# A mixture-of-experts block on one core: the light job of each pair first, the first job's flags counted early, the table inside job 0

## The reference

```python
def grouped_moe(x, w_router, router_bias, w_gate, w_up, w_down):
    scores = jax.nn.sigmoid((x @ w_router).astype(jnp.float32))
    ...
    gates = chosen / jnp.sum(chosen, axis=-1, keepdims=True)
    combine = jnp.einsum('btk,btke->bte', gates, jax.nn.one_hot(idx, N_EXPERTS, dtype=jnp.float32)).astype(x.dtype)
    y = jnp.zeros_like(x)
    for e in range(N_EXPERTS):
        h = jax.nn.silu(x @ w_gate[e]) * (x @ w_up[e])
        y = y + combine[..., e:e + 1] * (h @ w_down[e])
    return y
```

## Time and profile before

| | before |
|---|---|
| runs | 1537.62 us median of 3 (1533.61 to 1541.21) |
| the profiled execution | 1539.95 us, span 1538.0 us |
| granted TensorE clock, mean over the span | 0.924 |
| instructions recorded | 19449 |
| TensorE busy | 1301.7 us (85%) |
| VectorE, ScalarE, GpSimd busy | 430.4, 143.8, 76.2 us |
| moved by DMA | 559.43 MB, mean 364 GB/s |

### The profile page before, as it was taken

One profiled execution on the slowest core, in us unless ns is written; L12 is line 12 of the kernel. 1 busy time (PEld: TensorE's weight loads), 2 busy tenths in 40 slices (PEclk: granted clock), 3 DMA queues, 4 the chain that ended last, 5 costly groups with the idle time before them and its releaser, 6 DMA issues.

```text
span 1538.0 us, 19449 instructions
## 1 busy us (share of the span) xinstructions
PE 1301.7 (85%) x7868; PEld 540.2 (35%) x7869; DVE 430.4 (28%) x808; ACT 143.8 (9%) x252; POOL 76.2 (5%) x138
## 2 busy tenths in 40 slices
PE   3899999899998989799899899786787688687666
PEld 2556544455454564233233233122122122122121
DVE  3213694767557150012011111111111110101102
ACT  3000101323100123000000000000000000000000
POOL 0112100111131000000000000000000000000000
PEclk9999999899999879899999899998898898898867
DMA  9999668556888559879999999999999999999995
GB/s 373 420 388 409 259 261 336 183 203 234 317 346 298 203 196 422 340 285 399 422 422 422 421 422 421 422 421 421 421 422 422 422 422 422 421 422 421 422 420 245
DMA packets 84355, 559.43 MB, mean 364 GB/s; under 512 B 9680, under 2 KB 9680, under 8 KB 22608
## 3 DMA queue, kind: packets, MB, share of 16 engines
q1 hardware_dynamic: 69408, 502.49, 80.1%
q0 software_dynamic: 14320, 52.01, 9.2%
q10 hardware_dynamic: 576, 4.19, 0.7%
HBM read 556.57 MB, written 2.10 MB: 363 GB/s over the span
## 4 chain that ended last, share of the span: by engine, by line
PE 46%; DMA 44%; DVE 4%; issue 2%; ACT 2%; SPq 1%; DVEq 0%; ACTq 0%; POOL 0%
DMA ring<-w_gate_dram 16%; DMA ring<-w_up_dram 16%; PE ps L831 7%; PE ps L568 7%; PE ps L826 7%; DMA rope_heads<-w_down_dram 5%; PE ps L671 3%; DMA ring<-w_half_dram 3%; PE ps L858 3%; DMA ring<-w_in_dram 3%; PE ps L562 3%; PE ps L852 2%; PE ps L801 2%; PE ps L573 2%; PE ps L789 1%
## 5 line engine op out<-in xcount | busy, mean ns | idle before, releaser
L826 PE MATMUL ps<-ring,early 128*32 128x256 f32 x2304 | 179.4, 448 | 75.9 <-DMA ring<-w_gate_dram 32.3
L831 PE MATMUL ps<-ring,early 128*64 128x512 f32 x672 | 165.0, 613 | 27.8 <-DMA ring<-w_gate_dram 18.2
L1509 DVE TENSOR_TENSOR big<-ps,big 128x1024 f32<-128x1024 f32 x64 | 75.4, 1220 | 324.4 <-PE ps L789 324.4
L568 PE MATMUL ps<-ring,big 128*128 128x512 f32 x320 | 147.0, 601 | 0.0
L826 PEld LDWEIGHTS ps<-ring,early 128*32 128x32 f32 x2304 | 73.1, 123 | 195.5 <-issue 64.8
L1149 DVE SCALAR_TENSOR_TENSOR halves<-ring,silu_c,halves 128x1024 f32<-128x1024 f32 x96 | 123.2, 1283 | 39.6 <-DMA ring<-w_half_dram 33.3
L671 PE MATMUL ps<-ring,big 128*128 128x512 f32 x256 | 114.5, 604 | 1.3 <-ACT big L1034 1.3
L831 PEld LDWEIGHTS ps<-ring,early 128*64 128x64 f32 x672 | 41.5, 138 | 135.4 <-issue 64.9
L568 PEld LDWEIGHTS ps<-ring,big 128*128 128x128 f32 x320 | 59.2, 192 | 69.6 <-issue 69.4
L671 PEld LDWEIGHTS ps<-ring,big 128*128 128x128 f32 x256 | 48.8, 194 | 59.8 <-issue 59.8
L789 PE MATMUL ps<-halves,early 64*128 64x512 f32 x256 | 66.8, 642 | 0.0
(11 more groups left out here) (327 smaller groups left out, 1067.5 us busy)
## 6 DMA issues: line engine op xcount, KB each, us to landing
ring<-w_gate_dram SPq DMA_DIRECT2D x128, 1024.0 KB, 26.0
ring<-w_up_dram SPq DMA_DIRECT2D x64, 1024.0 KB, 26.0
ring<-w_down_dram SPq DMA_DIRECT2D x64, 1024.0 KB, 27.2
ring<-w_half_dram POOLq DMA_DIRECT2D x96, 512.0 KB, 6.5
ring<-w_mix_dram SPq DMA_DIRECT2D x32, 1024.0 KB, 12.0
big<-w_up_dram SPq DMA_DIRECT2D x32, 1024.0 KB, 26.0
big<-w_down_dram SPq DMA_DIRECT2D x32, 1024.0 KB, 25.3
ring<-w_in_dram SPq DMA_DIRECT2D x28, 1024.0 KB, 9.2
```

The lines of the kernel that those rows point to most:

```text
L568: mm = pe.matmul(ps[:, b + t, :], nT[:, k, t * P:(t + 1) * P], w, start=(k == 0), stop=(k == KT - 1))
L826: mm = pe.matmul(out_b[0][BASE * f:BASE * (f + 1), :], rows[0][:, k, :], w[:, kk, f * 256:(f + 1) * 256], start=(k == 0), stop=(k == KT - 1))
L831: mm = pe.matmul(out_b[1][REST * f:REST * (f + 1), :], rows[1][:, k, :], w[:, kk, f * N:(f + 1) * N], start=(k == 0), stop=(k == KT - 1))
L1509: tt(y, banks[:, 2 * h:2 * h + 2, :].rearrange("p a n -> p (a n)"), y, ALU.add).then_inc(done, 1)
```

## The change

It has four parts. In each pair of jobs the few job stands in front (TensorE's loops and the numbering on VectorE are changed together). Job 0's flags few and some come from a count of their own: two more small matmuls in route step 1, two operations on VectorE into two new places of `n_i`, and a step ("kind",) behind k = 9 in which TensorE reads them into registers. The table's matmuls move out of the schedule into `experts`, between gate and up of job 0, and write to the bank T; route steps 2 and 3 stand behind k = 7 and 11. Waits move with them: SyncE's wait of chunk 11 is for cand_ready, and for table_ready only behind chunk 23; TensorE waits for table_ready after job 0; job 0 waits for two gathered blocks at each gate chunk instead of all 16 at its start; the counts of the pairs are read one by one where they are used.

```diff
--- before.py
+++ after.py
@@ -101,8 +101,10 @@
     seq += [("hT", 3), ("logits", 3), ("gate_b", 0), ("gate_b", 1), ("route", 1)]
     for k in range(KT):
         seq.append(("first", k))
-        if k in (4, 8, 12):
-            seq.append(("route", 1 + k // 4))
+        if k in (7, 11):
+            seq.append(("route", 2 if k == 7 else 3))
+        if k == 9:
+            seq.append(("kind",))
     return seq
 
 
@@ -207,7 +209,7 @@
         bufB = sb("bufB", [P, 1024])
         probs = sb("probs", [P, 2, N])
         small = sb("small", [P, 64])
-        n_i = sb("n_i", [1, 4 * JOBS + 5], I32)
+        n_i = sb("n_i", [1, 4 * JOBS + 7], I32)
         hsq = sb("hsq", [P, TT, 4])
         onehot_j = sb("onehot_j", [CAND, JOBS])
         vcol = sb("vcol", [CAND, 10])
@@ -343,7 +345,7 @@
         outs_saved = [sem("outs0_saved"), sem("outs1_saved")]
         out_ready, out_sent = sem("out_ready"), sem("out_sent")
         dve_step, spread_saved = sem("dve_step"), sem("spread_saved")
-        sort_done = sem("sort_done")
+        sort_done, first_kind = sem("sort_done"), sem("first_kind")
 
         block = stack.enter_context(nc.Block())
 
@@ -400,13 +402,14 @@
                 elif i == 10:
                     sp.wait_ge(mask_ready, 1)
                 elif i == 11:
-                    sp.wait_ge(table_ready, 1)
+                    sp.wait_ge(cand_ready, 1)
                 if i < SLOTS:
                     sp.wait_ge(slot_free, used_job(i - SLOTS))
                 elif i >= JOB_SLOTS:
                     sp.wait_ge(slot_free, used_job(i - JOB_SLOTS))
                 sp.dma_start(job_slots[i % JOB_SLOTS], weights[i // 8][FIRST_EXPERT, i % 8]) \
                     .then_inc(job_landed[i % JOB_SLOTS], 16)
+            sp.wait_ge(table_ready, 1)
             jobs = sp.value_load(n_i[0:1, 4 * JOBS:4 * JOBS + 1], min_val=2, max_val=JOBS - 1)
             with sp.Fori(1, jobs) as j:
                 e = sp.value_load(n_i[0:1, bass.ds(j, 1)], min_val=0, max_val=NE - 1)
@@ -716,6 +719,9 @@
                         for t in range(TT):
                             mm = pe.matmul(T[0:CAND, 128:129], cand[:, t, 0, :], ones[:, 0:1],
                                            start=(t == 0), stop=(t == TT - 1))
+                        for t in range(TT):
+                            pe.matmul(T[0:1, 130:131], cand[:, t, 0, FIRST_EXPERT:FIRST_EXPERT + 1], ones[:, 0:1],
+                                      start=(t == 0), stop=(t == TT - 1))
                         pe.wait_ge(shift_ready, 1)
                         pe.matmul(T[:, 2 * NE:3 * NE], ones, rt[:, 18, 0, :], start=True, stop=True).then_inc(pos_done, 1)
                     elif part == 2:
@@ -732,21 +738,11 @@
                                 mm = pe.transpose(C[0][0:CAND, (2 * t + i) * P:(2 * t + i + 1) * P],
                                                   cand[:, t, i, :], ident)
                         mm.then_inc(candT_done, 1)
-                    else:
-                        pe.wait_ge(table_oh, 2)
-                        for i in range(2):
-                            for t in range(TT):
-                                at = (i * TT + t) * JOBS
-                                pe.matmul(Z[0][:, at:at + JOBS], candT[:, t, i, :], onehot_j[:],
-                                          start=True, stop=True)
-                        pe.matmul(Z[0][0:1, 256:256 + JOBS], k_("expert")[0:CAND, :], onehot_j[:],
-                                  start=True, stop=True)
-                        pe.matmul(Z[0][0:1, 256 + JOBS:256 + 2 * JOBS], vcol[:, 3:4], onehot_j[:],
-                                  start=True, stop=True)
-                        pe.matmul(Z[0][0:1, 256 + 2 * JOBS:256 + 3 * JOBS], vcol[:, 9:10], onehot_j[:],
-                                  start=True, stop=True)
-                        pe.matmul(Z[0][0:1, 256 + 3 * JOBS:256 + 4 * JOBS], vcol[:, 4:5], onehot_j[:],
-                                  start=True, stop=True).then_inc(table_done, 1)
+                elif kind == "kind":
+                    pe.wait_ge(first_kind, 1)
+                    first_few, first_some = (
+                        pe.value_load(n_i[0:1, 4 * JOBS + 5 + i:4 * JOBS + 6 + i], min_val=0, max_val=1)
+                        for i in range(2))
                 elif kind == "first":
                     k = step[1]
                     if k == 0:
@@ -772,6 +768,17 @@
                                            start=True, stop=True)
                     mm.then_inc(bcast_done, 1)
 
+            def table():
+                pe.wait_ge(table_oh, 2)
+                for i in range(2):
+                    for t in range(TT):
+                        at = (i * TT + t) * JOBS
+                        pe.matmul(T[:, at:at + JOBS], candT[:, t, i, :], onehot_j[:], start=True, stop=True)
+                for i, column in enumerate((k_("expert")[0:CAND, :], vcol[:, 3:4], vcol[:, 9:10], vcol[:, 4:5])):
+                    mm = pe.matmul(T[0:1, 256 + i * JOBS:256 + (i + 1) * JOBS], column, onehot_j[:],
+                                   start=True, stop=True)
+                mm.then_inc(table_done, 1)
+
             def scatter(j, t, banks=Yb):
 
                 if t == 0:
@@ -809,17 +816,19 @@
                     return job_slots[i % JOB_SLOTS]
 
                 rows = [xg[:, :, REST:BLK] if 1 in parts else xg[:, :, 0:BASE], xg[:, :, 0:REST]]
-                if first:
-                    pe.wait_ge(first_saved, KT)
-                else:
+                if not first:
                     pe.wait_ge(xg_ready, j)
                     if 1 in parts:
                         pe.wait_ge(outs_saved[0], j)
                 for m, out_b in ((0, Gb), (1, Ub)):
-                    if m == 1 and not first:
+                    if m == 1 and first:
+                        table()
+                    elif m == 1:
                         scatter(j, 0)
                     for i in range(8):
                         w = arrived(8 * m + i).rearrange("p (k f) -> p k f", k=2)
+                        if first and m == 0:
+                            pe.wait_ge(first_saved, 2 * i + 2)
                         for kk in range(2 if 0 in parts else 0):
                             k = 2 * i + kk
                             for f in range(4):
@@ -860,14 +869,12 @@
                                        w[:, q * N:(q + 1) * N], start=(i == 0), stop=(i == 7))
                     mm.then_inc(slot_free, 1)
 
-            pe.wait_ge(table_ready, 1)
-            jobs = pe.value_load(n_i[0:1, 4 * JOBS:4 * JOBS + 1], min_val=2, max_val=JOBS - 1)
-
             def any_job(j, first):
-                few = pe.value_load(n_i[0:1, JOBS:JOBS + 1] if first else n_i[0:1, bass.ds(j + JOBS, 1)],
-                                     min_val=0, max_val=1)
-                some = pe.value_load(n_i[0:1, 3 * JOBS:3 * JOBS + 1] if first else n_i[0:1, bass.ds(j + 3 * JOBS, 1)],
-                                     min_val=0, max_val=1)
+                if first:
+                    few, some = first_few, first_some
+                else:
+                    few, some = (pe.value_load(n_i[0:1, bass.ds(j + i * JOBS, 1)], min_val=0, max_val=1)
+                                 for i in (1, 3))
                 with pe.If(few):
                     experts(j, (0,), first)
                 with pe.Else():
@@ -877,6 +884,7 @@
                         experts(j, (0, 1), first)
 
             any_job(0, True)
+            pe.wait_ge(table_ready, 1)
 
             def count(i):
                 return pe.value_load(n_i[0:1, 4 * JOBS + i:4 * JOBS + i + 1], min_val=0, max_val=JOBS - 1)
@@ -884,15 +892,18 @@
             def loop(start, end):
                 return nc.Fori(start, end, engines=bass.OrderedEngineSet([pe.engine]), hint_back_edge=True)
 
-            many_pairs, pairs, mid_pairs, rest = count(1), count(2), count(3), count(4)
+            many_pairs = count(1)
             with pe.If(many_pairs):
                 with loop(0, many_pairs) as i:
-                    experts(i * 2 + 1, (0, 1))
-                    experts(i * 2 + 2, (0,))
+                    experts(i * 2 + 1, (0,))
+                    experts(i * 2 + 2, (0, 1))
+            pairs, mid_pairs = count(2), count(3)
             with pe.If(mid_pairs):
                 with loop(many_pairs, pairs) as i:
-                    experts(i * 2 + 1, (1,))
-                    experts(i * 2 + 2, (0,))
+                    experts(i * 2 + 1, (0,))
+                    experts(i * 2 + 2, (1,))
+            rest = count(4)
+            jobs = pe.value_load(n_i[0:1, 4 * JOBS:4 * JOBS + 1], min_val=2, max_val=JOBS - 1)
             with pe.If(rest):
                 with loop(pairs * 2 + 1, jobs) as j:
                     any_job(j, False)
@@ -1418,6 +1429,9 @@
                 last = ts(oh_first[:, t, :], k_("slots")[:, 0:BLK], rt[:, 19, t, FIRST_EXPERT:FIRST_EXPERT + 1],
                           small[:, 10 + t:11 + t], ALU.is_equal, ALU.mult)
```

(18 more changed lines are left out.)

## The result

The changed kernel takes 1508.92 us, the median of 4 runs (1508.04 to 1514.08), against 1537.97 for the kernel before (4 runs, 1533.61 to 1541.21). The ratio is 0.9832 with a 95% interval of 0.9807 to 0.9857: 25.8 us of 1537.97, or 22.0 to 29.7, faster; the two medians themselves lie 29.1 apart, inside that interval. Forecast were 22.0. The profiled execution took 1514.08, the slowest of the four, with a span of 1512.3, 25.7 less than the one profiled before. The runs of one kernel spread by 6 to 8 us here, so that these 25.7 match the 25.8 to a tenth is chance.

A forecast was written before the change was run, and what follows sets the result against it. The stream of weights was taken to set the end. Terms -22.1 (hole), +1.5 (dip) and -1.4 (start of job 0) gave -22.0 us, from 1537.62 to 1515.6, said as 1516; range 1511 to 1527.

The forecast's parts named there:

- The bound and the hole: Expert stage: the weight stream sets the end; 22.1 us of it lost from 615 to 710 should return through the order.
- The dip: Start of job 1: the slots still run dry briefly behind job 0, costing 1.5 us, bounds 0 and 5.7.
- The start of job 0: Ahead of job 0: table, last evacuation and loads leave the path, new loads and matmuls join: -1.4 us, bounds +0.6 and -2.2.
- The table's term: Ahead of job 0: the table's matmuls leave the path, -1.28 us.
- rope_heads' slot: SyncE's issue after cand_ready instead of table_ready, from 563.75 to about 554: gains 0 by itself, bounds 0 and -0.5.
- Table inside job 0: Between gate and up of job 0: the table's 1.28 us are covered by 1.9 us of waits for w_up, cost 0.
- Rival A: Behind job 0: the gap grows because TensorE jumps over unused variants that now hold a table; 1520 or 1526, chance 0.09.
- Both stops that I named: TensorE's 9.22 us gap behind job 0 and a 4.68 us stop inside the last job, each after a jump.
- the rule that it cites: Trainium skill: a taken branch beyond the loaded window forces a fetch first; by it both stops remain as they are.
- B: Job 2 doesn't start level with the stream; a lag of 16 us gives -16, 1522; chance 0.04.
- C: At the end: the last pair's mid job, at a low clock with a stop, finishes late: 3 us slower, 1541; chance 0.03.
- D: No measurable change: a hole opens elsewhere and the 22 us don't reach the end; about 1538, chance 0.05.

The follow-up runs named there:

- e1: The kernel before with only the new order in the pairs (few job first; loops and VectorE's numbering): 1515.6 us, ratio 0.9881 against the kernel before.
- e2: The changed kernel with the old order in the pairs turned back, all else as changed: 1525.8 us, ratio 0.9943 against the kernel before.
- e3: The changed kernel with all four counts read into registers at once right behind job 0: 1509.15 us, ratio 0.9831 against the kernel before.
- e8: The kernel before with counts read late and three unused register loads ahead of job 0, putting the loops' code back in place: 1538.43 us, ratio 1.002.
- e12: The changed kernel with the table's matmuls back in the schedule, behind the gather of k = 13: 1513.42 us in one run.
- e7: The changed kernel with route steps 2 and 3 back behind k = 4 and 8: 1512.86 us in one run.
- e6: The changed kernel with SyncE again waiting for the table (table_ready) before chunk 11: 1524.14 us in one run.
- e5: The changed kernel with job 0's few variant standing last, so the jump comes before job 0: 1511.78 us, ratio 0.9833 against the kernel before.
- e11: The changed kernel with 55 register loads in a job 0 variant that never runs, moving only code: 1522.46 us, ratio 0.9908 against the kernel before.
- e9: The changed kernel with gathers from k = 4 and route steps 2 and 3 inside job 0, few variant last: 1512.0 us, ratio 0.9841 against before.
- e10: The changed kernel with gathers from k = 4 and route steps 2 and 3 inside job 0, few variant first: 1505.98 us, ratio 0.9818 against before.

## Why the prediction came out as it did

**The bound and the hole: right.** The stream sets the end, and the 22.1 us lost between 615 and 710 came back: 420 GB/s there. e1 and e2 show that the order does it, by 18.9 and 15.6 us.

**The dip: 1.5 forecast, 0 measured.** The working behind it held: before, the slots run dry at 629.0, 61.7 us behind the restart, and e1, with the long gap, near 623.9, 61.6 behind its own, with a dip of 2.7. In the changed kernel that point is 624.9, and the first slot is free at 620.20. What failed is the length of the gap: 8.3 forecast, 4.27 measured. I priced it by register loads, and a load costs 0.63 to 0.67 (e3, e8) instead of 0.3; but the bulk is fetches of code: two packets in the gap of before, one in that of the changed kernel. With one load each, the gap is 4.3 in e2 and 9.1 to 9.2 in e8 and e12. That the changed kernel has only one is luck: nothing in the prediction aimed at it.

**The start of job 0: -1.4 forecast, -4.1 measured** (567.30 to 563.23), beyond my bound of -2.2. The table's term, -1.28, I leave as it was: it had no wait in front of it in the kernel before. A term was missing: the placing of the route steps, which I had priced at nothing, is worth 1.4 (e7). And one was mis-sized: I had the stop before job 0 shrink by 1.2 and the new loads cost 0.7, net -0.5; the whole stop of 1.51 is gone and the loads don't show, since the gathers queued ahead of them cover them. -1.28 - 1.4 - 1.51 and +0.2 for the later first gather give -4.0. Of these the 1.4 has an experiment of its own; the 1.28 and 1.51 are read from the two timelines.

**rope_heads' slot: 0, right** in the form forecast, and e6 shows what hangs on it (11.6 us). **Table inside job 0: 0, right.** From its first matmul to its last job 0 takes 51.97 us (562.10 to 614.07) against 51.92 before, and TensorE still waits 0.6 us for an up chunk, with the table's matmuls done at 570.5.

**The tail: not in the sum, -0.9 measured.** Behind the last chunk the matmuls of L796 from 1500.86 take 2.82 us at a granted clock of 0.70, where those of before (L789, 1525.65) take 3.79 at 0.51. The prediction had no such term, and no part of the change aims at it: it is luck. e1, e3 and e5 have it too (17.4 to 17.5 us behind the last chunk), e7 and e12 don't (18.5).

The misses in the start and the dip, 2.7 and 1.5 us, both point to faster; with no dip the stream should have won 22.1 and won 20.8, which takes 1.3 back, and the tail gives 0.9: 22.0 + 2.7 + 1.5 - 1.3 + 0.9 = 25.8.

**Rival A** (a stop for code) didn't happen in the changed kernel, but its mechanism is real: a stop of 2.5 to 3.5 us in each round, 12.5 us in all, once the code lies badly (e11). I had argued that ten more matmuls barely lengthen the jump; its length isn't what counts (e11's is 165 instructions longer, with a gap of 4.13), the place of the code is. The kernel before and the changed one both lie well, which I hadn't planned. Both stops that I named are fetches of code (packets at 618.6, 624.3 and 1464.7), but they don't remain as they were, as the prediction had it by the rule that it cites: the gap fell from 9.22 to 4.27, and in place of the 4.68 the changed kernel stops for 1.70 ahead of its last job (1437.51). **B, C and D** didn't come: job 2 starts level, since the last chunk of job 1 makes TensorE wait 1.40 us for its transfer (656.59); the last job waits for its chunks (1494.77); no other hole opens (422 GB/s from 710 to 1480).

## What to carry to other kernels

Where a stream of weights sets the end, look for the one place where its rate falls while the compute engine is full, and ask what it met with full buffers: put the job that is cheaper than its own transfer there, and let the dear ones start level with the stream. A stop of the compute engine is free while slots are still being filled; count chunks from the restart to find when they run dry, and lay jumps and sorts inside that time. In a kernel with loops and branches on the device, look at the packets of the instruction queue first whenever an edit moves the time without a reason: moving nine instructions cost 0.96% here.

## What the runs showed of the hardware

- Where code lies costs time. 55 register loads that never run (165 instructions) made the kernel 12.5 us slower from the first gather (11.7 by the ratios): TensorE's loop over pairs then fetched 9 packets of 16 KB in a round of 122 us, where the changed kernel fetches none from 707 to 978. Stops in it end 2.5 us behind the start of a packet. The rule by which a loop fits wasn't worked out.
- A jump over unused code stops TensorE for 2.9 to 3.3 us ahead of job 0 (e5, e9). Behind job 0 the stop is 2.1 to 4.4 us with one packet (6.2 with three more loads) and 9.1 to 9.6 with two. It is 2.1 to 2.4 where the packet starts while matmuls still run (e6, e10).
- The granted clock rises 4.7 to 6.6 us behind the first gather where two route steps stand behind gathers 7 and 11, and 9.2 to 9.9 where they stand behind 4 and 8; that is worth 1.4 us (e7).
- A register load on TensorE costs 0.63 to 0.67 us where nothing covers it, and nothing where matmuls are queued ahead of it: the two of the changed kernel leave no stop in its gathers or ahead of job 0.
- The stages ahead of the experts vary from run to run: the first gather begins between 542.4 and 550.5 in kernels whose code up to it is the same but for a few small matmuls.
